# Three weight splits moved on VectorE and ScalarE, and the gate-weight sums of each group made by GpSimd, in a two-layer encoder kernel

## What is computed

```python
for i, y_i in enumerate((ya, yb, yc)):
    z = cols(COL_Z + i * BRANCH_WIDTH, BRANCH_WIDTH)
    g = cols(COL_G + i * D_MODEL, D_MODEL)
    u = jax.nn.sigmoid(g) * ((y_i * jax.nn.silu(z)) @ w_br[i])
    merged = u if merged is None else merged + u
out = merged @ w_out
return x + gate[:, None, :] * out
```

## Time and profile before

| | us |
|---|---|
| median of three runs | 2354.3 (2353.31 to 2354.72) |
| the profiled execution's own time | 2358.96 |
| its span, first to last instruction | 2357.2 |
| PE busy | 2311.8 (98% of the span) |
| DVE busy | 1621.2 (69%) |
| ACT busy | 1122.9 (48%) |
| POOL busy | 58.7 (2%) |
| mean granted TensorE clock | 0.997 |

### The profile page before, as it was taken

How to read it: one execution, slowest core, us unless ns; L and a number is a source line. 1 busy time by engine, 2 the same in 40 slices (tenths; PEclk the granted TensorE clock), 3 DMA queues, 4 the chain that set the end, 5 groups by cost and what they waited for, 6 DMA issues and landing times.

```text
span 2357.2 us, 41870 instructions
## 1 busy us (share of the span) xinstructions
PE 2311.8 (98%) x15466; PEld 2141.9 (91%) x15466; DVE 1621.2 (69%) x4481; ACT 1122.9 (48%) x3035; POOL 58.7 (2%) x103
## 2 busy tenths in 40 slices
PE   7999999999999999999999999999999999999999
PEld 5888888999999899999888889989999997999998
DVE  7877567577776575676578856775787765666762
ACT  5666457444444443334346664663444434443340
POOL 0010011000000000000001001100000000000000
PEclk9999999999999999999999999999999999999999
DMA  7221321121111322221520112112111122222223
GB/s 280 95 75 37 115 78 50 64 83 58 48 61 38 117 79 63 103 94 64 164 79 35 44 44 95 39 50 99 50 59 37 59 82 81 81 90 77 87 83 121
DMA packets 63034, 186.11 MB, mean 79 GB/s; under 512 B 9584, under 2 KB 22512, under 8 KB 59888
## 3 DMA queue, kind: packets, MB, share of 16 engines
q1 hardware_dynamic: 52320, 164.00, 20.1%
q10 hardware_dynamic: 10512, 19.44, 2.3%
HBM read 168.73 MB, written 12.58 MB: 77 GB/s over the span
## 4 chain that ended last, share of the span: by engine, by line
PE 88%; DVE 5%; ACT 4%; issue 2%; DMA 1%; SPq 0%; ACTq 0%; DVEq 0%
PE ps_proj L987 58%; PE ps_score L1031 8%; PE ps_pt L1031 6%; PE ps_score L1164 2%; PE ps_pt L1177 2%; PE ps_pv L1213 2%; PE ps_score L1148 1%; PE ps_tr L1228 1%; PE ps_pv L1194 1%; PE ps_tr L1229 1%; PE ps_pv L1207 1%; ACT act_hi L1438 1%; DMA w_raw<-in_w 1%; DVE top L2028 1%; DVE w_lo L2314 1%
## 5 line engine op out<-in xcount | busy, mean ns | idle before, releaser
L987 PE MATMUL ps_proj<-w_hi,act_hi 128*128 128x384 f32 x1824 | 632.6, 347 | 3.3 <-ACT act_hi L1438 2.2
L987 PE MATMUL ps_proj<-w_hi,act_lo 128*128 128x384 f32 x1824 | 612.2, 336 | 0.0
L987 PE MATMUL ps_proj<-w_lo,act_hi 128*128 128x384 f32 x1824 | 611.8, 335 | 0.0
L987 PEld LDWEIGHTS ps_proj<-w_hi,act_hi 128*128 128x128 f32 x1824 | 342.8, 188 | 9.2 <-ACT act_hi L1438 5.8
L987 PEld LDWEIGHTS ps_proj<-w_lo,act_hi 128*128 128x128 f32 x1824 | 343.4, 188 | 0.0
L987 PEld LDWEIGHTS ps_proj<-w_hi,act_lo 128*128 128x128 f32 x1824 | 342.5, 188 | 0.0
L1957 DVE TENSOR_REDUCE ssq<-square 128x2 f32<-128x256 f32 (+1 forms) x228 | 95.6, 419 | 215.5 <-ACT square L1532 214.8
L1532 ACT ACTIVATE square<-ps_proj 128x256 f32<-128x256 f32 x228 | 88.2, 387 | 271.3 <-PE ps_proj L987 270.7
L2314 DVE TENSOR_TENSOR w_lo<-w_raw,w_hi 128x1536 fp32r<-128x1536 f32 (+3 forms) x121 | 188.5, 1559 | 11.2 <-ACT w_hi L1362 10.6
L1362 ACT ACTIVATE w_hi<-w_raw 128x1536 fp32r<-128x1536 f32 (+2 forms) x120 | 161.0, 1342 | 58.4 <-DMA w_raw<-in_w 37.4
L987 PE MATMUL ps_proj<-act_hi,w_hi 128*128 128x512 f32 (+1 forms) x512 | 174.6, 341 | 8.1 <-DVE w_lo L2314 4.7
(11 more groups left out here) (263 smaller groups left out, 4898.1 us busy)
## 6 DMA issues: line engine op xcount, KB each, us to landing
w_raw<-in_w SPq DMA_DIRECT2D x80, 768.0 KB, 5.1
w_raw<-in_w SPq DMA_DIRECT2D x40, 512.0 KB, 3.7
s_raw<-in_w_gate SPq DMA_DIRECT2D x72, 256.0 KB, 3.0
w_ada<-in_w_mod SPq DMA_DIRECT2D x11, 1536.0 KB, 6.6
wb_raw<-in_w_branch SPq DMA_DIRECT2D x24, 512.0 KB, 3.5
first_ada<-in_w_first SPq DMA_DIRECT2D x8, 1024.0 KB, 12.8
parked<-y_t ACTq DMA_DIRECT2D x4, 1536.0 KB, 7.1
w<-in_w_gate SPq DMA_DIRECT2D x24, 256.0 KB, 3.9
```

The lines of the kernel that those rows point to most:

```text
L987: op = pe.matmul(out, sta[s](k), mov[m](k), start=(k == 0 and n == 0), stop=(k == chunks - 1 and n == 2))
```

## The change

Four edits:

1. The high part of the first swish piece of C is made one unit later by ScalarE (unit 142 for 141 in layer 0, 437 for 436 in layer 1), and with it its low part on VectorE (143 for 142, 438 for 437).
2. The low parts of the other three swish pieces of C stand at the top of their `z` units' bodies, ahead of `gate` and `gated_low`, not behind them.
3. The low parts of the second and third output piece are made three units behind their high parts, not one: at units 284 and 285 for 282 and 283 (579 and 580 for 577 and 578).
4. `combine` and its table are gone from VectorE; GpSimd makes T1 to T4 in `combos`, in the order T1, T2, T3, T4, each as soon as its quarters are there and the product that last read its buffer is done.

```diff
-COMBO_AT = {5: ("T1",), 6: ("T2", "T3"), 8: ("T4",)}
...
+        if p[0] == "z" and p[2:] == ("C", 0):
+            before = FIRST_USE[p] - 2
...
+LOW_IN = {n + (3 if p[0] == "o" and p[2] in (1, 2) else 1): p for n, p in SPLIT_IN.items()}
...
+            def combos(g):
+                before = group_before(g)
+                def free(c):
+                    if before:
+                        pool.wait_ge(*proj_ready.at(product(before, c)))
+                    elif PLACE[c] < 6:
+                        pool.wait_ge(*proj_ready.at(UNITS[LAST_USE[BEFORE_GROUPS[g[0]][PLACE[c] // 3]]]))
+                def combine(c, first, second_):
+                    pool.tensor_tensor(s_raw[PLACE[c]][:], first[:], second_[:], ALU.subtract
+                                       ).then_inc(*combo_ready.inc((g, c)))
+                free("T1")
+                pool.wait_ge(*quarter_in["W12"].at(g))
+                pool.wait_ge(*quarter_in["W11"].at(g))
+                combine("T1", w12, s_raw[PLACE["W11"]])
...
             for n, u in enumerate(UNITS):
+                if u[0] == "z" and u[2:] == ("C", 2):
+                    combos(groups_of(u[1])[0])
+                if u[0] == "s" and u[4] == 0 and not last_group(group_unit(u)):
+                    combos(group_after(group_unit(u)))
...
+                if n in LOW_IN and u[0] == "z" and u[2] == "C":
+                    low_part(LOW_IN[n])
...
-                        for c in COMBO_AT.get(at, ()):
-                            combine(group_after(g), c)
...
-                if n - 1 in SPLIT_IN:
-                    low_part(SPLIT_IN[n - 1])
-                if u[0] == "z" and u[2:] == ("C", 2):
-                    for c in COMBOS:
-                        combine(groups_of(l)[0], c)
+                if n in LOW_IN and not (u[0] == "z" and u[2] == "C"):
+                    low_part(LOW_IN[n])
```

More of the change, by code:

```diff
@@ L364 @@
 SPLIT_IN = split_slots()
+LOW_IN = {n + (3 if p[0] == "o" and p[2] in (1, 2) else 1): p for n, p in SPLIT_IN.items()}
+assert len(LOW_IN) == len(SPLIT_IN)
 SPLIT_ORDER = [p for n in range(len(UNITS)) for p in
@@ L974, in biases @@
                     op.then_inc(*bias_ready.inc((l, h, part)))
+            def combos(g):
[12 more added lines that the diff above has]
+                combine("T1", w12, s_raw[PLACE["W11"]])
+                free("T2")
+                pool.wait_ge(*quarter_in["W22"].at(g))
+                pool.wait_ge(*combo_ready.at((g, "T1")))
+                combine("T2", s_raw[PLACE["W22"]], s_raw[PLACE["T1"]])
+                free("T3")
+                combine("T3", s_raw[PLACE["W22"]], w12)
+                free("T4")
+                pool.wait_ge(*quarter_in["W21"].at(g))
+                pool.wait_ge(*combo_ready.at((g, "T2")))
+                combine("T4", s_raw[PLACE["W21"]], s_raw[PLACE["T2"]])
             pool.wait_ge(later_in, 16 * 4)
             for n, u in enumerate(UNITS):
+                if u[0] == "z" and u[2:] == ("C", 2):
+                    combos(groups_of(u[1])[0])
+                if u[0] == "s" and u[4] == 0 and not last_group(group_unit(u)):
+                    combos(group_after(group_unit(u)))
                 if u[0] == "q" and u[5] == 5 and (u[2] == "B" or u[2:4] == ("A", 3)) and u[2:4] != ("B", 3):
@@ L2193, in add_up @@
                     dve.tensor_tensor(kept1[:], sum_bank(u), kept1[:], ALU.add).then_inc(*summed.inc((g, "C21")))
[L2195 to L2215, removed]
-                dve.tensor_tensor(s_raw[PLACE[c]][:], first[:], second_[:], ALU.subtract
-                                  ).then_inc(*combo_ready.inc((g, c)))
             def s_low(g, c):
```

## The result

The changed kernel takes 2360.3 us in the median of ten runs (2358.85 to 2361.47), the kernel before 2354.93 in ten (2353.31 to 2358.37). The ratio is 1.0022, 95% interval 1.0013 to 1.0030: 3 to 7 us slower. The forecast was 2345.5, with a range up to 2353.5, and a chance of 0.05 for a kernel that is slower.

What follows compares the result with a forecast made beforehand. The prediction took TensorE, busy 98% of the span, as the bound, with gains only in its waits and clock falls. Terms -1.3 + 1.8 - 3.9 - 5.4 + 0 = -8.8 us from 2354.3 gave 2345.5, range 2342.5 to 2353.5.

Steps and rivals of the forecast that it cites:

- the three moves: First swish piece, later swish low parts and output low parts moved later or earlier: -1.3 + 1.8 - 3.9 - 5.4 us.
- The sums on GpSimd: Groups: 96 VectorE instructions go to GpSimd at 1.2 us each; ordinary groups lose nothing, parked groups just fit: 0.
- 0.72 of its length: VectorE loses 0.72 of a GpSimd instruction's length, from one `crossed` that took 1.015 us for 0.418.
- Rival C: Parked groups: VectorE stands still for a whole GpSimd sum, 1.1 us late in each of four; 2349.9 us, chance 0.14.
- The first move: First swish piece one unit later, before the first swish unit: +0.4 in layer 0, -1.65 in layer 1, clock +1.8.
- one fall in two: Clock falls after one of the two new `w_lo` waits ahead of the first swish units: +1.8, bounds 0 and 3.6.
- The later swish pieces: Low parts ahead of the gate at the third and fourth pieces: four waits of 1.07 us go, -4.28 + 0.35 = -3.9.
- what is late next: Later swish pieces: the gate, behind 1.22 us of low part, frees a PSUM bank about 0.35 us late in layer 0.
- The outputs: Output pieces' low parts later: 2 x (-1.14 - 1.8) + 0.45 = -5.4 us, from shorter `act_lo` waits and clock.
- The clock term: Outputs: with shorter `act_lo` waits the clock no longer falls, -1.8 us a layer, 0 if it still falls.
- The 4.7 us between the two are the same in both kernels: Whole kernel: gap between profiled execution (2358.96) and median (2354.3) taken as unchanged, so the sum is subtracted from the median.
- Rival E: Parked groups: GpSimd sums of 2 us stop VectorE throughout and the clock falls after each; 2366 us, chance 0.05.

Runs made afterwards that it cites:

- the sums alone: The changed kernel with all three moves undone, so only the sums on GpSimd: ratio 1.0028, +6.6 us against the kernel before.
- The run with sums beside ordinary groups only: Kernel before with 72 of 96 sums and the first group's on GpSimd, those due beside C0, A0, B0 on VectorE, no move: ratio 0.9998.
- The subtraction and the fill beside the sums: Kernel before plus small GpSimd subtractions at the four sums' places (ratio 1.0037), or zero fills there instead (0.9996); VectorE keeps its sums.
- the moves alone: The changed kernel with the sums back on VectorE, so only the three moves: ratio 0.9995, -1.2 us against the kernel before.

## Why the prediction was wrong

The forecast missed by 14.8 us (2360.3 for 2345.5). Two steps hold it: the sums, a term put at 0 that is 6.6, and the three moves, put at -8.8 where they bring -1.2, which is another 7.6. The first was a wrong reading of where VectorE has room, the second clock terms and waits taken from one execution and subtracted in full from a median, and a gate that, once later, holds up the first group.

**The sums on GpSimd, forecast 0, measured +6.6 alone.** Three things failed in this step:

- The price of a sum was near: 1.26 us is the least that the record has, 1.3 to 1.7 the medians, 2.02 the most, since a sum too waits for VectorE. I had 1.2, bounds 0.69 and 1.65, and had named over 1.65 as a sign of failure.
- The stop was mis-sized. "0.72 of its length" came from one instruction that need not have begun with its neighbour; in A0 the stops are 1.1, 0.5, 1.1 and 1.1 us. Rival C had it right that the stop is a full one: the VectorE instruction stands until the sum is done. Three stops of 2.7 us in all stood against a spare time of 2.5, and that is only 0.3 late at the matmul named; the other 0.6 comes from the fourth stop, on the `s_lo` that stands ahead of `part`. I had counted the stops up to `yz_lo` and not followed VectorE's queue to the next thing that TensorE waits for.
- The first groups were not looked at. I wrote that ordinary groups lose nothing and that only A0 and B0 are tight. The first group of each layer is as tight: before, its first `sum` ended at 860.01 and TensorE took up the bank at 860.07. In the changed kernel T1 stands beside the `s_lo` ahead of that sum (1.77 for 0.68), and with the chain already late by the moves TensorE waits 1.69: 1.7 to 1.9 us a layer. With the sums alone T1 costs nothing there, and 0.85 a layer is lost later in the group, at `merged`. Before, and changed:

```profile
859.46 0.55 DVE L2178 TENSOR_TENSOR sum<-ps_pt,kept 128x384 f32<-128x384 f32 x1
...
860.07 0.44 PE L1031 MATMUL ps_pt<-mix_hi,s_hi 128*128 128x384 f32 x1
```

```profile
859.16 1.39 POOL L990 TENSOR_TENSOR s_raw<-w,s_raw 128x512 f32<-128x512 f32 x1 [41.36 <-DMA s_raw<-in_w_gate]
...
859.33 1.77 DVE L2238 TENSOR_TENSOR s_lo<-s_raw,s_hi 128x512 fp32r<-128x512 f32 x1
...
861.02 0.55 DVE L2214 TENSOR_TENSOR sum<-ps_pt,kept 128x384 f32<-128x384 f32 x1
...
861.62 0.44 PE L1067 MATMUL ps_pt<-mix_hi,s_hi 128*128 128x384 f32 x1 [1.69 <-DVE sum L2214]
```

A TensorE that didn't wait for 270 us was read as room. It says nothing on how near VectorE was to being late. The run with sums beside ordinary groups only shows that where there was room there was enough, and that the six groups without it hold the whole loss. The rule of the Trainium skill ("SBUF — State Buffer", section "Who interferes with whom"), cited in the prediction for rival C, has that a VectorE instruction with two SBUF inputs contends with a GpSimd instruction that reads SBUF, and not with one that only writes. The subtraction and the fill beside the sums agree with both halves: 737 against 684 ns, and 684.

**The first move, forecast +0.5 with its clock, measured +1.9 alone and about +4 beside the others.** Against the execution of the rows its waits were forecast well: +0.5 and -1.6 in the ledger for +0.4 and -1.65. The clock was not: I charged one fall in two, and it fell after 5 of 6 waits of 2.27 us. In layer 1 the fall of before, at the wait for `mod_row`, is part of the -1.6; it came back at the wait for `w_lo`, so there it only moved. And the -1.65 itself was an accident of that execution. It rests on a wait of 2.33 us for `mod_row` and on matmuls at half clock; the other traces of the old order waited 1.3 to 2.0 there, most of them at full clock, and against these the move loses some 0.5 us in layer 1 too, before any fall.

**The later swish pieces, forecast -3.9.** The four waits went: -1.02, -0.37, -1.05 and -1.16 in the ledger, -3.6. The step that failed is "what is late next": the gate, later by a low part, leads into the first group's chain on VectorE, where TensorE waits 0.6 us a layer (the moves alone have the same wait with GpSimd making no sums). The 220 matmuls of the swish units took 38.4 to 39.1 us in layer 0 and 38.2 in layer 1 and take 36.7 to 37.2 and 35.9; the first group takes 0.8 more in each. So the move is worth some 2.5, an estimate.

**The outputs, forecast -5.4, measured -4.0 alone.** At full clock the stage of layer 1 is 1.2 to 1.3 us shorter, for 1.14 worked out, and the 0.45 at the first output's last step in layer 0 is there as a wait of 0.44; the waits on `act_lo` went from 3.4 only to 1.8. The clock term was mis-sized: 1.8 a layer was read off the granted clock of the profiled execution, where a fall cost 1.3 and 1.5, and the fall comes in 4 of 14 stages, which is some 0.8 us for both layers and not 3.6.

**The frame of the sum.** "The 4.7 us between the two are the same in both kernels" was wrong. The profiled execution had three falls of the clock at 1.3 to 1.7 us each, where the traces of this order have about one; the two more are some 3 us, an estimate, of the 4 by which it stood above the median. The median holds only the share of a fall that comes in most executions, so subtracting a fall from it in full takes off time that isn't there. Its 2358.96, over 4 us above each of the three runs then known (2353.31 to 2354.72), should have said so.

In sum: the sums +6.6 for 0, the moves -1.2 for -8.8; the two add up to 5.4, and the changed kernel has +5.2. Rival C had the right rule and, for the parked groups, nearly the right size (1.1 us each, measured 0.9 to 1.0), but no loss in the first groups. Rival E, the slower side, put a sum at 2 us and a fall of the clock behind each parked group; most sums took 1.3 to 1.7, and the clock stayed up in the groups.

## What to carry to other kernels

Work moved to an idle GpSimd is not free for VectorE: in these runs a subtraction of GpSimd that reads SBUF could stop a VectorE instruction with two SBUF operands until it was done, and the place to look is not VectorE's load but the few spots where TensorE takes its result with tenths of a microsecond to spare, followed down the queue. A bottleneck engine without waits shows no slack of its suppliers; measure that from the end of the supplier's instruction to the start of the reader. And a fall of the clock in one profiled execution is a chance, not a cost: weigh it by how many executions show it, and don't subtract it from a median.

## What the runs showed of the hardware

- A GpSimd subtraction of 128x512 float32 takes 1.26 us at the least, against 0.69 on VectorE; of 128x224, 0.56 us at the least, 0.85 in the mean beside a busy VectorE. A fill of 128x224 takes 0.285 us, busy VectorE or not.
- The two engines stop each other: beside VectorE the same sums take up to 2.02 us in the changed kernel, and 2.27 with the sums alone, where the `wb_lo` beside one took 2.31 for 1.22.
- The granted clock went to its lower level after 5 of 6 waits of 2.27 us, after 4 of 14 pairs of waits of 1.09 and 0.59, and after 0 of 14 pairs of about 0.5 and 0.4. In the 23 us around the last adaLN units of layer 1 in nine traces with the old place of the high part it fell in 3, after waits of 2.33, 2.01 and 1.79, and not after 1.83 or less in the other six; of second executions of two of these it fell in one, after 1.91, and not in the other, after 1.64. One fall costs 1.3 to 1.5 us in the outputs and 1.6 at the first swish units.
